# Centring the values of a recurrent layer in another stage, with one wide matmul, and turning half of them by transposing matmuls

## What is computed

```python
z = z + mu_prev * (z_prev - z) + mu_next * (z_next - z)
r, k, v, wd, ad, gd = split(z)
# 16 heads of 64; per head a state S of 64 x 64, over the tokens, forwards and backwards:
sk = einsum('bhvk,bhk->bhv', S, kh_t)
S = S * w_t - sk[..., None] * ak_t + v_t[..., None] * kt_t
o_t = einsum('bhvk,bhk->bhv', S, r_t)
o = layernorm(o_f + o_b, gn_g, gn_b)          # over the 64 features of a head
bonus = sum(r * (kt_f + kt_b) * r_k) * v
out = (o + bonus) * g
```

## Time and profile before

| | us |
|---|---|
| median of 3 runs | 3234.85 (3233.75 to 3237.01) |
| the profiled execution | 3245.93 |
| its span in the trace | 3243.7 |
| PE busy | 3136.3 (97%) |
| DVE busy | 1916.9 (59%) |
| ACT busy | 1051.5 (32%) |

### The profile page before, as it was taken

The page is one execution under the profiler, slowest core; times in us unless marked ns, Lnnn a source line. Parts: engine busy times, 40 slices in busy tenths (PEclk is TensorE's granted clock), DMA queues, the critical chain, the costliest instruction groups (busy, mean ns, idle before and its releaser), DMA issues. The chain is left out here.

```text
span 3243.7 us, 61223 instructions
## 1 busy us (share of the span) xinstructions
PE 3136.3 (97%) x26250; PEld 2100.3 (65%) x26250; DVE 1916.9 (59%) x3037; ACT 1051.5 (32%) x1717; POOL 372.1 (11%) x236
## 2 busy tenths in 40 slices
PE   9999999999999999989999999999999999999997
PEld 4564665455555577677777777677666666666664
DVE  2337762667776599646566565655554455545446
ACT  2337662334433236533433441003311211321111
POOL 0000000000000263200000233334200001300002
PEclk9999999999999999999999999999999999999998
DMA  3212101334454523365555423411122122122111
GB/s 142 59 47 61 47 23 54 125 126 133 145 178 138 195 85 111 132 204 165 170 167 151 166 92 123 151 65 59 59 78 72 59 75 75 56 93 85 62 62 65
DMA packets 225980, 336.98 MB, mean 104 GB/s; under 512 B 56113, under 2 KB 184497, under 8 KB 218673
## 3 DMA queue, kind: packets, MB, share of 16 engines
q1 hardware_dynamic: 225712, 333.08, 31.7%
HBM read 230.13 MB, written 96.34 MB: 101 GB/s over the span
## 5 line engine op out<-in xcount | busy, mean ns | idle before, releaser
L656 PE MATMUL ra_ps<-xT,ring 128*128 128x512 f32 (+1 forms) x1152 | 429.8, 526 | 0.0
L2410 PE MATMUL tl_ps<-merged,pool 128*128 128x320 f32 x1440 | 405.1, 433 | 2.7 <-PEq L108 2.1
L2410 PEld LDWEIGHTS tl_ps<-merged,pool 128*128 128x128 f32 x1440 | 273.6, 190 | 118.9 <-issue 4.7
L656 PEld LDWEIGHTS ra_ps<-xT,ring 128*128 128x128 f32 x1152 | 214.3, 190 | 198.9 <-issue 189.3
L2673 DVE TENSOR_TENSOR oR<-tl_ps,oR 128x320 f32<-128x320 f32 x416 | 202.3, 490 | 152.7 <-PE tl_ps L2410 149.9
L2495 ACT ACTIVATE ring<-tl_ps 128x320 f32<-128x320 f32 x96 | 42.0, 437 | 533.7 <-PE tl_ps L2410 533.7
L2410 PE MATMUL tl_ps<-hold,pool 128*128 128x320 f32 x720 | 202.6, 432 | 0.0
L2679 DVE TENSOR_TENSOR merged<-tl_ps,ring 128x320 f32<-128x320 f32 x96 | 47.2, 492 | 255.4 <-PE tl_ps L2410 140.3
L2410 PE MATMUL tl_ps<-xT,pool 128*128 128x320 f32 x640 | 182.7, 432 | 0.0
L2410 PEld LDWEIGHTS tl_ps<-hold,pool 128*128 128x128 f32 x720 | 136.8, 190 | 57.0
L2410 PE MATMUL tl_ps<-merged,sums 128*128 128x320 f32 x544 | 162.6, 438 | 5.8 <-DVE oR L2671 3.2
(11 more groups left out here) (338 smaller groups left out, 5434.9 us busy)
## 6 DMA issues: line engine op xcount, KB each, us to landing
pool<-ub SPq DMA_DIRECT2D x320, 160.0 KB, 2.8
ub<-ra_ub SPq DMA_DIRECT2D x32, 1280.0 KB, 5.3
pool<-in_w_ff SPq DMA_DIRECT2D x32, 1024.0 KB, 4.8
pool<-in_w_ff SPq DMA_DIRECT2D x64, 512.0 KB, 3.5
ring<-in_w_in SPq DMA_DIRECT2D x38, 512.0 KB, 3.6
pool<-in_w_merge SPq DMA_DIRECT2D x15, 1024.0 KB, 4.9
ub<-ra_v SPq DMA_DIRECT2D x16, 640.0 KB, 6.4
xT<-in_xT SPq DMA_DIRECT2D x15, 640.0 KB, 7.2
```

Source lines behind the costliest of these rows:

```text
L656: last = pe.matmul(ps[:, bank + j, 0:n], w[c][:, 128 * i:128 * i + 128], xT[:, i, t0:t0 + n], start=(i == 0), stop=(i == KT - 1))
L2410: last = pe.matmul(bank(n, b), lhs(k), rhs(k), start=(fresh and k == 0), stop=(k == d - 1), skip_group_check=True)
```

## The change

A new constant, 128x128, holds the identity minus 1/64 within each of two blocks of 64, so that one matmul centres both heads of a pair. In the scaled stage PE applies it to v in three pieces (`centre_values`, into bank 5), and ACT copies each piece back over v (`values_out`). Pieces 0 and 1 go after `lower(p - 1, 0, 3)` and after `low_piece(p, 0, 2)`, piece 2 after `lower(p - 1, 1, 6)`. SP sends v to `ub` after this, in the next pair's turn and behind a wait. In the state stage `values` takes the identity in place of `centre`, and for h = 1 it is a transposing matmul.

```diff
+C_CEN2 = C_CEN + 64
+NCONST = C_CEN2 + 128
+    c[:, C_CEN2:C_CEN2 + 128] = np.eye(128) - (p[:, None] // 64 == p[None, :] // 64) / CH
@@ scaled stage, SP
                     send_half(p - 1, 1, 1)
+                    sp.wait_ge(vc_done, 3 * p)
+                    for d in range(2):
+                        sp.dma_start(hbm["ub"][p - 1, d][:, :, 0:CH], v[:, :]...).then_inc(v_sent, 16)
...
-                if p < PAIRS:
-                    sp.wait_ge(mix_s[2], p + 1)
-                    sp.wait_ge(mix_p[2], p + 1)
-                    for d in range(2):
-                        sp.dma_start(hbm["ub"][p, d][:, :, 0:CH], v[:, :]...).then_inc(v_sent, 16)
@@ scaled stage, PE
+            def centre_values(p, j):
+                t0, n = SPANS[j]
+                pe.wait_ge(bonus_done, p + 1)
+                after(pe, vc_done, 3 * p + j if j else 0)
+                pe.matmul(ps[:, 5, 0:n], cst[:, C_CEN2:C_CEN2 + 128], v[:, t0:t0 + n], start=True, stop=True).then_inc(vc_ready, 1)
                     lower(p - 1, 0, 3)
+                    pe.wait_ge(mix_p[2], p)
+                    centre_values(p - 1, 0)
                 after(pe, mix_p[2], p)
                 span(0, 0, 2)
                 low_piece(p, 0, 2)
+                if p:
+                    centre_values(p - 1, 1)
...
                     lower(p - 1, 1, 6)
+                    centre_values(p - 1, 2)
                 span(1, 3, 1)
                 low_piece(p, 1, 0)
+                after(pe, vc_done, 3 * p)
                 span(1, 3, 2)
...
             whole(0, 0).then_inc(gate_ready, 1)
+            pe.wait_ge(bonus_done, PAIRS)
+            centre_values(PAIRS - 1, 0)
             lower(PAIRS - 1, 0, 6)
+            centre_values(PAIRS - 1, 1)
             for j, (t0, n) in enumerate(SPANS):
+                if j == 1:
+                    centre_values(PAIRS - 1, 2)
                 if j == 2:
                     lower(PAIRS - 1, 1, 6)
+                    pe.wait_ge(vc_done, 3 * PAIRS)
@@ scaled stage, ACT
+            def values_out(p, j):
+                act.wait_ge(vc_ready, 3 * p + j + 1)
+                act.activation(seg(v, j), ps[:, 5, 0:SPANS[j][1]], ACT.Copy).then_inc(vc_done, 1)
                     lower_out(p - 1, 0)
+                    values_out(p - 1, 0)
                 scale_own(p, 0, k, 1)
                 sigmoids(p, 0, 2)
                 if p:
+                    values_out(p - 1, 1)
                     lower_out(p - 1, 1)
+                    values_out(p - 1, 2)
...
                 if c:
+                    values_out(PAIRS - 1, 2)
                     lower_out(PAIRS - 1, 1)
                 act.activation((tq, rs)[c][:, :], set_of(ps, 3 * c), ACT.Sigmoid).then_inc(gate_done, 1)
                 if c == 0:
+                    values_out(PAIRS - 1, 0)
                     lower_out(PAIRS - 1, 0)
+                    values_out(PAIRS - 1, 1)
@@ state stage, PE
             def values(g, u):
                 for h in range(2):
-                    last = pe.matmul(ps[other(h), UB, CH * u:CH * u + CH], ub[g % 3][half(h), u, 0:CH], centre[half(h)],
-                                     start=True, stop=True)
+                    if h:
+                        last = pe.transpose(ps[other(h), UB, CH * u:CH * u + CH], ub[g % 3][half(h), u, 0:CH], ident64[half(h)])
+                    else:
+                        last = pe.matmul(ps[other(h), UB, CH * u:CH * u + CH], ub[g % 3][half(h), u, 0:CH], ident64[half(h)], start=True, stop=True)
```

More of the change, by code:

```diff
@@ L36 @@
 C_CEN = C_ID64 + 64
-NCONST = C_CEN + 64
+C_CEN2 = C_CEN + 64
+NCONST = C_CEN2 + 128
 (P_MP, P_MN, P_W0, P_A0, P_KK, P_KA, P_RK, P_GG, P_GB) = (0, 3, 6, 8, 10, 11, 12, 13, 14)
@@ L547, in scaled_stage @@
         lz_ready, l_own, l_mixed, l_tanh = st.sems("lz_ready l_own l_mixed l_tanh")
+        vc_ready, vc_done = st.sems("vc_ready vc_done")
         gate_ready, gate_done, l1_copied = st.sems("gate_ready gate_done l1_copied")
@@ L610, in _ @@
                     send_half(p - 1, 1, 1)
+                    sp.wait_ge(vc_done, 3 * p)
+                    for d in range(2):
+                        sp.dma_start(hbm["ub"][p - 1, d][:, :, 0:CH], v[:, :].rearrange("p (c n) -> p c n", n=CH)).then_inc(v_sent, 16)
                 if 0 < p < PAIRS - 1:
@@ L636, in _ @@
                     sp.dma_start(w[2][:, :], hbm["w_in"][B_LOW + 2]).then_inc(ahead[2], 16)
-                if p < PAIRS:
-                    sp.wait_ge(mix_s[2], p + 1)
-                    sp.wait_ge(mix_p[2], p + 1)
-                    for d in range(2):
-                        sp.dma_start(hbm["ub"][p, d][:, :, 0:CH], v[:, :].rearrange("p (c n) -> p c n", n=CH)).then_inc(v_sent, 16)
             gate_out(1)
```

## The result

| | before, us | after, us |
|---|---|---|
| median, same chip | 3235.93 (4 runs, 3233.75 to 3241.17) | 3333.06 (4 runs, 3325.85 to 3340.74) |
| the profiled execution | 3245.93 | 3325.85 |
| its span | 3243.7 | 3323.7 |

The changed kernel takes 1.0281 times as long [1.0264, 1.0299]. It is slower, as forecast, but by 97 us and not by 12: far outside the range of 3237 to 3267. The two profiled executions lie 80 us apart, because the one of before is above the median of its runs and the one of after is the fastest of four. The other three of after had a lower mean granted clock (0.982 to 0.987, against 0.988), and the four times stand in the order of their clocks.

A forecast was written before the change was run, and what follows sets the result against it. PE was taken to bound the kernel, in the state stage by turns through matmuls and instruction supply. 17.2 + 0.5 + 1.4 + 0 - 7 = +12.1 us on 3234.85 gave 3247.0 us, range 3237 to 3267.

The forecast's parts named there:

- what a transposing call costs: State stage, PE: 0.055 us for 64 columns, no extra gap at the change of kind, hidden under L1635's quarter, so nothing.
- Rival (a): State stage: transposing matmuls don't run beside their neighbours, 18 to 87 us; at 0.1 us each, 32 us, 3279; 15%.
- the quoted rule: Trainium skill, array packing restrictions: column tiling switches the float32 transpose mode off; cited as speaking against the change.
- The pauses: State stage, PE stops between pieces of 256 instructions: 640 instructions fewer were taken as -7 us, bounds 0 and 12.
- rival (b): State stage: the pauses shrink by far more, gain 12.6 us or more, kernel not slower; 14%, 3% for faster.
- Both signs of being wrong: State stage: L1635's group has grown; pauses have lost more than 12 us. Either would show the prediction wrong.
- 17.2 us for the matmuls: Scaled stage, PE: three added matmul calls a pair, 2.15 us for each of 8 pairs, all on the path.
- the 0.5 for entries and waits: Scaled stage, PE: entering and leaving blocks costs nothing visible; 24 new waits, 0 to 0.1 us each, 0.5 us together.
- ACT's copies: Scaled stage: three copies from PSUM a pair, some 1.6 us, hidden in the loop with 2.8 us clear, so no cost.
- The one stall forecast: End of the scaled stage: PE waits 1.4 us at piece 1 for ACT's copy of piece 0, behind the sigmoid.
- Rival (c): Scaled stage: ACT's copies hold PE up in all 24 places by about 0.7 us, 17 us more, 3264; 7%.
- SP's moved transfers: Scaled stage: v's two transfers go later, behind a wait on SP's queue; taken as 0, at most 2 us.

The follow-up runs named there:

- e1_plain: The changed kernel with a plain matmul by the identity for both heads in `values`, centring kept in the scaled stage; 3266.96 us, 1.0085 times the kernel before.
- e3_fewer: The kernel before, without the h = 1 matmuls of `values` from step 1 on (1248 loads and matmuls fewer); 3219.78 us, 0.9942 times the kernel before.
- e2_grouped: The changed kernel with a step's eight transposing calls in one row behind the group, ahead of the scores; 3253.55 us, 1.0043 times the kernel before.
- e7_two_rows: The changed kernel with a step's transposing calls in two rows of four, behind units 3 and 7; 3257.38 us in one execution.

## Why the prediction was wrong

The direction was right for the scaled stage's sake: e1_plain, with nothing of the transposing calls, is already 1.0085. The size was wrong for the state stage's.

**The step that failed** is the one on what a transposing call costs: "so the change of kind leaves no extra gap ... It lies under L1635's quarter and costs nothing." It costs 2.30 us in each of 40 steps, 92 us.
The price could have been read beforehand. In the earlier trace rows the last start of `values` beside L1635 is 1397.38 and the first score 1397.54: 0.16 us against a spacing of 0.06 within the row, at a change from quarter to half. Two such changes in 320 places are, as an estimate, 320 x 2 x 0.15 = 96 us, close to the 92 measured. I looked at the earlier trace rows for the price of a mixture that the earlier trace rows show better.

**Rival (a)** had the mechanism ("if the array has to be empty before or while it runs"), and its upper bound was 87 us. Its point value, 0.1 us each, and its 15% were both too low: measured are 2.30 / 8 = 0.29 us each, slightly over its upper bound of 0.27. I set the value near to the earlier trace rows although the quoted rule was said to make this the likeliest; the range then ended inside the rival. (The cost at which (a) leaves the forecast's 3256 is 9 / 320 = 0.03 us each, not 0.02.)

**The pauses** were read rightly and priced too low. Predicted: -7 us, bounds 0 to 12. e3_fewer measures 16.7 ns for each instruction, so 640 fewer are worth 10.7 us, the case in which every piece is at the limit. What the step left out is that pauses also give way to array time. A piece that takes longer on the array than 4.14 us leaves no pause behind, and with 11.80 us a step the array is above the 10.1 in which the instructions arrive. So in the changed kernel the pauses went from 45.0 to 3.7 us, and 41 of the 92 us were swallowed. So rival (b) came true in the pauses and not in the time: it said "PE needs the array time anyway", and here PE needed far more of it. Both signs of being wrong that the trace could show, the grown group and over 12 us less of pauses, are there. In the table every kernel's mean step lies 0.2 to 0.35 us above the larger of its two limits.

**The clock** was not in the sum. By the traces' records of the granted clock, PE stood at half clock (1.2 GHz) for 8 us of the state stage before and for 40 us after; the shares of the windows, 0.99 of 434 us and 0.96 of 495 us, say the same. The windows of 16 us at the start of the stage, in the changed kernel and in e2_grouped, which runs the same transposes in a row:

```profile
1414.00:1430.00 16.00, 16.00 (x240) 11.73 (x238) 3.60 (x8) 4.78 (x10) 0.00 (x0) 0.64 0.77 245
```

```profile
1414.00:1430.00 16.00, 14.47 (x430) 12.35 (x428) 8.04 (x18) 6.42 (x14) 0.00 (x0) 1.00 0.94 289
```

The changed kernel got through 240 matmuls, at a mean clock of 0.64, where the other did 430. At half clock a unit takes 0.65 us instead of 0.44. From these an estimate: 40 us at half clock hold the work of 27, so they cost some 13 us, and the 8 of before some 3. The steps give somewhat less: the mean one is 0.33 longer than an undisturbed one, 39 x 0.33 = 13 us, of which 3.7 are pauses and some 9 are left.

What lowers the clock these runs do not settle. All four executions of the changed kernel have a mean clock of 0.982 to 0.988 and those of the other kernels 0.989 to 0.994 (the one of 7536.57 us aside), so a lower clock does go with the changed kernel. But the state stage of e1_plain, without a transposing matmul, has 22 us at half clock, that of e7_two_rows 11 and that of e2_grouped 3: one trace of each says little on why.

The state stage's account, with 8 to 10 us more than before for the clock as an estimate: 92 - 41 + 8 to 10 = 59 to 61, and 59.5 measured.

**Scaled stage.** The centring matmuls, PE's timeline in pair 1 of after (L699 is `centre_values`); the earlier trace rows are the same stretch before:

```profile
625.31 1.89 PE L684 MATMUL ra_ps<-ra_ub 64*32 64x32 f32 x160
627.13 1.13 PE L699 MATMUL ra_ps<-ra_v,cst 128*128 128x512 f32 x2
628.09 3.62 PE L656 MATMUL ra_ps<-xT,ring 128*128 128x256 f32 x16
631.64 0.70 PE L668 MATMUL ra_ps<-low,ra_lw 64*128 64x256 f32 x4
632.27 1.12 PE L699 MATMUL ra_ps<-ra_v,cst 128*128 128x512 f32 x2
633.23 7.03 PE L656 MATMUL ra_ps<-xT,ring 128*128 128x512 f32 x16
```

The same `lower` of the next pair, after and before:

```profile
693.53 1.90 PE L684 MATMUL ra_ps<-ra_ub 64*32 64x32 f32 x160
```

```profile
691.71 1.89 PE L684 MATMUL ra_ps<-ra_ub 64*32 64x32 f32 x160
```

A pair takes 693.53 - 625.31 = 68.22 us and took 691.71 - 625.63 = 66.08: 2.14 more in this pair, 2.15 in the next two, the price read from L72 to within 0.01. A piece of 512 columns does take 0.96 from start to start, where columns alone give 0.86, but the block behind it is 0.1 shorter (628.09 to 631.64, 3.55, against 3.66 before). So 17.2 us for the matmuls hold, and the 0.5 for entries and waits was not there.

From the fourth pair on the difference grows to 2.4 and more. PE stops at 833.92, 902.00, 970.80, 1039.63 and 1110.17, for 0.14, 0.13, 0.85, 1.38 and 0.78 us in which neither a matmul nor a load runs, where the kernel before has no such stop. The third and the fourth, as the timeline has them (with the idle time of the matmuls alone):

```profile
970.80 1.24 PE L656 MATMUL ra_ps<-xT,ring 128*128 128x256 f32 x5 [0.85 <-issue]
```

```profile
1039.63 1.02 PE L699 MATMUL ra_ps<-ra_v,cst 128*128 128x512 f32 x2 [1.50 <-issue]
```

In PE's program, counted with its waits, these five places lie exactly 1,024 instructions apart, four pieces of 256, and e1_plain, e2_grouped and e7_two_rows stop at the last three of them too. They are the same pauses as in the state stage, here behind or in `lower` with its 320 loads and matmuls in 1.5 us. A pair has 1,028 instructions where it had 1,013, so the places fall otherwise than before; that this is why the stops came is likely and not shown. The prediction had the pauses in one stage and priced none in the other: they are the 4 us that 17.2 leaves of 21.3.

ACT's copies do nothing to PE in the loop, as said. The answer on L814 has them with nobody who waits:

```profile
L814 ACT ACTIVATE ra_v<-ra_ps x24: 384/597/598, 628.3 to 1118.9; 128x512 f32<-128x512 f32 x16, 128x256 f32<-128x256 f32 x8
```

The one stall forecast, at the end of the stage, did not come as forecast. `lower` and piece 1 on PE:

```profile
1107.92 1.48 PE L684 MATMUL ra_ps<-ra_ub 64*32 64x32 f32 x149
1110.17 0.31 PE L684 MATMUL ra_ps<-ra_ub 64*32 64x32 f32 x11 [0.78 <-issue]
1110.41 1.13 PE L699 MATMUL ra_ps<-ra_v,cst 128*128 128x512 f32 x2
```

From `lower` to what follows it is 2.49 us and was 1.51: 1.0 where I had 1.4. But the stop stands before `lower`'s last 11 matmuls, at the fifth of the places above, so it is a pause and not the wait for ACT. The copy is out at 1110.23; without the pause PE would have been at piece 1 at 1107.92 + 1.51 = 1109.43 and waited 0.8 us, which the pause covers. (The 1.4 was also summed wrongly: piece 0 has 512 columns and takes 0.86, not 0.43, which leaves 1.0.) Rival (c) did not occur; SP's moved transfers, put at 0, cost nothing that can be seen.

## What to carry to other kernels

Before a new kind of matmul goes in the midst of packed small ones, look up in which form of the array it can run, and price every change of form from the nearest place in the trace where the form already changes (here 0.14 to 0.17 us each way), times the number of changes: eight calls in a row cost 0.42 us here, the same eight spread out 2.30. Where PE stops at regular places with its operands ready, count its instructions as a second limit beside the array's time: taking instructions away gains only what that limit holds, and added array time costs only what exceeds it. When a rule of the Trainium skill speaks for a rival and no row speaks against it in the same form, the rival is the forecast.

## What the runs showed of the hardware

The change of form between quarters (64x64) and half rows with all columns stands as 0.15 us on the way in and 0.14 to 0.17 on the way out, and each further pair of changes adds 0.27 us to the step, the same from one row (e2_grouped) to two (e7_two_rows, one execution) as on to eight (the changed kernel: 2.31 worked out, 2.30 measured). That this was so exact I had not expected.

PE's instructions arrive at 16.7 ns each where they are the limit (e3_fewer: 20.8 us for 1,248), and this stage of the kernel before ran at that limit and not at its array's: by undisturbed steps it would take 39 x (10.67 - 9.50) = 46 us less.

Such a limit can also show in a stage that looks bound by the array alone: the centring added 15 instructions to a pair of the scaled stage, where PE had been busy 560.20 of 561.00 us, and stops of up to 1.4 us appeared at every fourth piece of 256.
